# First attention stage: softmax weights made for two items at once, four buffers, the compressed branch and the weight split placed earlier

## The chip, the cores and the metric

The kernel runs on one core of one Trainium2 chip. The metric is the device time of one execution in microseconds (us), as the median of several runs. Engines are called by the profile's names or in words: PE is TensorE (PEld its weight loads), DVE is VectorE, ACT is ScalarE, POOL is GpSimd, SP issues the DMAs of the weight stream.

## The reference, cut to what matters

A model of four layers over 256 tokens of width 1024, all in float32: sparse attention, multi-head latent attention, a convolution layer and differential attention, with six feed-forward blocks. The change touches only the first mixer. There, 16 heads in 4 groups (head width 64) attend in three branches:

```python
s_c = einsum('bqghd,bjgd->bghqj', qb, k_cmp) * scale - slopes * (tf[:, None] - cmp_mid[None, :])
p_c = masked_softmax(s_c, cmp_end[None, :] <= t[:, None])          # 15 compressed blocks
o_c = einsum('bghqj,bjgd->bqghd', p_c, v_cmp)
...                                                                # selected branch o_s, window branch o_w
o = gb[..., 0:1] * o_c + gb[..., 1:2] * o_s + gb[..., 2:3] * o_w   # gates
return o.reshape(B, Q_BLOCK, NSA_HEADS * DH)
...
x = x + o @ w_out
```

k_cmp and v_cmp come from `compress`: 32 tokens with positions added, times w1, plus b1, gelu, times w2; k_cmp is then normed. With 256 tokens the selected and the window branch both see all earlier keys.

## The kernel before, in words

Every engine runs its own program in order; semaphores join them. All weights come as a stream of units of 3072 columns (piece a: 2048, piece b: 1024) into two slots of `raw`. ScalarE rounds a unit into `whi` (`hi_a`, `hi_b`) and VectorE takes the rest, raw minus hi, into `wlo` (`lo_a`, `lo_b`); TensorE multiplies three times (hi x hi, hi x lo, lo x hi) in `mm3`. Unit 10 is `U_OUT`, the first of three of the output projection; its operand is `hthi` and `htlo`, eight chunks of 128 rows, two heads each.

The first attention (`attention("nsa", ...)` on PE, ACT and DVE) is cut into 32 items, one for a head and a tile of 128 queries. `nsa_item(i)` gives head and tile: in each four, the first two are two heads with the first tile (128 keys, "short" below), the other two the same heads with the second tile (256 keys, "long"). An item goes: scores of both branches on TensorE (`nsa_scores`, two items at a time, four PSUM banks); `bias` on DVE adds slope times distance and finds the minimum (`near`, made by GpSimd per head); exp on ACT with the row sum (`lsum`); `probs` on DVE: reciprocal of two sums, product with two gates, scaling of both branches' weights; `transposes` on TensorE ("turning"); a copy on ACT into `n_pt`; `nsa_values` on TensorE for two items; and after each four a copy of the output (`post`, into `n_o`).

The loops on the three engines have index i. At i, DVE does bias(i) and probs(i-2); ACT does post, exp(i), the copy of item i-2; PE does, around transposes(i), scores of the pair two ahead and the values of the pair before. Tables (`besides`, `between`) written out by hand place other work at an index, after (on PE: before) that index's item work. In these tables are: the remaining keys and queries; the compressed branch, which is one chain over all three engines: hidden_taken, hidden_turned, hidden_biased, hidden_cubed, hidden_tanh, hidden_gelu, second_layer, key_root (a square root and two table loads), place_values, cmp_keys_normed, cmp_keys_turned, keys_placed, then for each tile t cmp_scores, cmp_biased, cmp_exp, cmp_weighted, cmp_turned, cmp_taken, and for each pair of chunks k cmp_values, branches_added, added_hi, added_lo; and the split of unit 10 (hi_a at 15, lo_a at 29). After the attention come cmp_values(3), the last additions and splits, and then TensorE waits until all eight chunks are split (`s_ol` at 8) before it starts unit 10. `busy` does nothing here (its count is 0).

The lines that the steps below touch: L681 exp, L690 copy of turned weights, L656 post, L797 hidden_biased, L808 to L810 key_root, L833 cmp_taken, L837 added_hi; L1342 transposes, L1377 scores, L1398 values, L1502 and L1505 second_layer, L1518 cmp_scores, L1540 cmp_values, L1037 to L1039 the projection; L1922 bias, L1954, L1955 and L1958 probs, L2079 to L2081 hidden_gelu, L2090 cmp_keys_normed; L465 near on GpSimd; L515 hi_a and L1708 lo_a.

## Time and profile before

| | |
|---|---|
| median of 3 runs | 1742.36 us (1740.43 to 1744.89) |
| the profiled execution | 1740.27 us, of which its span 1738.5 us |
| PE busy | 1666.1 us, 96% of the span |
| DVE, ACT, POOL busy | 1114.8, 809.4, 45.3 us |
| mean granted TensorE clock | 0.986 of full speed |
| first item's exp begins | 77.20 us |
| first matmul of the output projection | 163.97 us |
| stage between the two | 86.8 us, 5% of the span |

How to read it: an engine's row in a timeline has start, length, engine, line, operation, output and input and their sizes, the count merged, and in brackets how long the engine sat idle before and what released it. In the chain of work each row is start, length and what was running; the pieces follow each other until the end. Matmuls overlap, so that the distance between starts is less than a length. A clock of 0.5 means 1.2 GHz, 1.00 is 2.4 GHz.

### The profile page before, as it was taken

What the parts mean: (1) busy time and instruction counts of PE and PEld (TensorE: products, weight loads), DVE (VectorE), ACT (ScalarE), POOL (GpSimd) and SP (SyncE); (2) the same over time, 40 slices, a digit from 0 to 9 for tenths busy, and PEclk for the clock granted to TensorE, in tenths of its full rate; (3) what the DMA queues carried; (4) which work ended last, traced back from release to release, by engine and by line L of the source; (5) the groups of instructions that cost most, each with busy time, mean ns of one, the idle gap of its engine ahead of it and who ended that gap; (6) DMA issues with size and microseconds to landing.
All of it is one profiled execution on the core that took longest, in us unless ns stands there. A gap on an engine that the chain in (4) does not pass through costs nothing.

```text
span 1738.5 us, 30380 instructions
## 1 busy us (share of the span) xinstructions
PE 1666.1 (96%) x11793; PEld 1539.6 (89%) x11793; DVE 1114.8 (64%) x1735; ACT 809.4 (47%) x1236; POOL 45.3 (3%) x73
## 2 busy tenths in 40 slices
PE   8977999998999999999999999999999999899998
PEld 8856999987799999999997789999999999699997
DVE  4857766667666666766676476667666665676665
ACT  5575533346554334533352453335433354753333
POOL 0110000000000000000003010000000000000000
PEclk9988999998999999999999999999999999999999
DMA  7422454545046554444548255553555544045553
GB/s 268 161 71 86 166 197 181 183 155 179 28 147 230 215 217 181 182 181 181 184 162 243 71 191 191 191 190 141 201 184 190 191 166 150 17 167 203 189 187 145
DMA packets 56543, 293.92 MB, mean 169 GB/s; under 512 B 6720, under 2 KB 7232, under 8 KB 34080
## 3 DMA queue, kind: packets, MB, share of 16 engines
q1 hardware_dynamic: 52784, 280.61, 45.0%
q0 software_dynamic: 3696, 12.45, 2.4%
q8 instruction: 42, 0.69, 0.2%
q14 instruction: 21, 0.17, 0.0%
HBM read 290.95 MB, written 2.08 MB: 169 GB/s over the span
## 4 chain that ended last, share of the span: by engine, by line
PE 87%; DVE 6%; ACT 5%; issue 2%; DMA 0%; SPq 0%; DVEq 0%; ACTq 0%
PE bank L1037 18%; PE bank L1038 18%; PE bank L1039 18%; PE bank L1309 9%; PE bank L1278 4%; PE bank L1280 4%; PE bank L1282 4%; PE bank L1057 2%; PE bank L1608 1%; ACT att L704 1%; PE bank L1243 1%; PE bank L1245 1%; PE bank L1253 1%; PE bank L1342 1%; DVE wlo L1708 1%
## 5 line engine op out<-in xcount | busy, mean ns | idle before, releaser
L1037 PE MATMUL bank<-hthi,whi 128*128 128x256 f32 x2128 | 603.2, 283 | 2.1 <-DVE wlo L1714 2.1
L1038 PE MATMUL bank<-htlo,whi 128*128 128x256 f32 x2128 | 602.9, 283 | 0.0
L1039 PE MATMUL bank<-hthi,wlo 128*128 128x256 f32 x2128 | 602.9, 283 | 0.0
L1708 DVE TENSOR_TENSOR wlo<-raw,whi 128x2048 fp32r<-128x2048 f32 x171 | 391.8, 2291 | 96.4 <-ACT whi L515 96.4
L1037 PEld LDWEIGHTS bank<-hthi,whi 128*128 128x128 f32 x2128 | 408.7, 192 | 8.3 <-DVE wlo L1714 2.3
L1038 PEld LDWEIGHTS bank<-htlo,whi 128*128 128x128 f32 x2128 | 408.7, 192 | 4.7
L1039 PEld LDWEIGHTS bank<-hthi,wlo 128*128 128x128 f32 x2128 | 408.8, 192 | 0.0
L607 ACT ACTIVATE tr<-tr 128x256 f32<-128x256 f32 x132 | 55.1, 418 | 651.1 <-DVE tr L1801 651.1
L515 ACT ACTIVATE whi<-raw 128x2048 fp32r<-128x2048 f32 x171 | 326.4, 1909 | 31.0 <-PE bank L1039 29.2
L1801 DVE TENSOR_TENSOR tr<-bank,rb 128x512 f32<-128x512 f32 x132 | 91.2, 691 | 231.6 <-PE bank L1039 231.4
L1714 DVE TENSOR_TENSOR wlo<-raw,whi 128x1024 fp32r<-128x1024 f32 x171 | 208.4, 1219 | 22.0 <-ACT whi L523 21.3
L523 ACT ACTIVATE whi<-raw 128x1024 fp32r<-128x1024 f32 x171 | 178.2, 1042 | 0.4 <-PE bank L1039 0.3
L1037 PE MATMUL bank<-whi,hthi 128*128 128x384 f32 (+3 forms) x440 | 146.2, 332 | 8.0 <-DVE wlo L1714 3.7
L1038 PE MATMUL bank<-wlo,hthi 128*128 128x384 f32 (+3 forms) x440 | 144.3, 328 | 0.0
L1039 PE MATMUL bank<-whi,htlo 128*128 128x384 f32 (+3 forms) x440 | 144.2, 328 | 0.0
L1278 PE MATMUL bank<-whi,hidhi 128*128 128x512 f32 x288 | 113.3, 394 | 0.0
L1280 PE MATMUL bank<-wlo,hidhi 128*128 128x512 f32 x288 | 112.9, 392 | 0.0
L1282 PE MATMUL bank<-whi,hidlo 128*128 128x512 f32 x288 | 112.1, 389 | 0.0
L1804 DVE TENSOR_TENSOR tr<-tr 128x256 f32<-128x256 f32 x132 | 56.1, 425 | 63.8 <-ACT tr L607 63.8
L1309 PE MATMUL bank<-whi,hidhi 128*128 128x512 f32 x240 | 94.1, 392 | 0.0
L1309 PE MATMUL bank<-wlo,hidhi 128*128 128x512 f32 x240 | 94.1, 392 | 0.0
L1309 PE MATMUL bank<-whi,hidlo 128*128 128x512 f32 x240 | 93.4, 389 | 0.0
(281 smaller groups left out, 2004.2 us busy)
## 6 DMA issues: line engine op xcount, KB each, us to landing
raw<-in_stream SPq DMA_DIRECT2D x175, 1024.0 KB, 5.5
raw<-in_stream SPq DMA_DIRECT2D x176, 512.0 KB, 3.6
wide<-in_wide POOLq DMA_DIRECT2D x7, 512.0 KB, 4.1
tr<-in_taps POOLq DMA_DIRECT2D x6, 512.0 KB, 3.6
xn<-gated POOLq DMA_DIRECT2D x12, 142.0 KB, 3.0
proj<-gated POOLq DMA_DIRECT2D x8, 142.0 KB, 4.8
att<-gated POOLq DMA_DIRECT2D x8, 142.0 KB, 5.3
x<-in_x SPq DMA_DIRECT2D x2, 512.0 KB, 4.9
```

The costliest lines, as they stand in the source:

```text
L515: nc.scalar.activation(whi[:, s, 0:UA], raw[:, s, 0:UA], ACT.Copy).then_inc(s_hia, 1)
L523: nc.scalar.activation(whi[:, s, UA:UNIT], raw[:, s, UA:UNIT], ACT.Copy).then_inc(s_hib, 1)
L1037: nc.tensor.matmul(out, whi_, mhi, start=start, stop=False)
L1038: nc.tensor.matmul(out, whi_, mlo, start=False, stop=False)
L1039: return nc.tensor.matmul(out, wlo_, mhi, start=False, stop=stop)
L1278: nc.tensor.matmul(acc[2 * t + j][:, :], hidhi[:, b, lhs], whi[:, s, sl], start=start, stop=False, skip_group_check=True)
L1280: nc.tensor.matmul(acc[2 * t + j][:, :], hidhi[:, b, lhs], wlo[:, s, sl], start=False, stop=False, skip_group_check=True)
L1282: ins = nc.tensor.matmul(acc[2 * t + j][:, :], hidlo[:, b, lhs], whi[:, s, sl], start=False, stop=stop, skip_group_check=True)
L1309: ins = nc.tensor.matmul(acc[2 * t + j][:, :], a[:, 1, lhs], w[:, s, sl], start=False, stop=False, skip_group_check=True)
L1708: V.tensor_tensor(wlo[:, s, 0:UA], raw[:, s, 0:UA], whi[:, s, 0:UA].bitcast(F32), ALU.subtract)\
L1714: V.tensor_tensor(wlo[:, s, UA:UNIT], raw[:, s, UA:UNIT], whi[:, s, UA:UNIT].bitcast(F32), ALU.subtract)\
L1801: V.tensor_tensor(gu[:, j, :].rearrange("p (h n) -> p h n", h=2), gate_up_bank[j], both, ALU.mult)\
```

## The change

In the first attention alone:

- `n_sc` and `n_pr`, the buffers of biased scores and of weights, become four in place of three (short items get smaller ones), and every wait on them goes by four.
- `probs` of an item becomes `pair_probs` of two: one reciprocal over four sums and one product with four gates, then the four scalings; it runs at odd i for items i-3 and i-2.
- The compressed chain stands at earlier indices. The values of the second layer are copied once by ACT (`vraw`, ahead of them key_root), and GpSimd makes the four masked copies `vz`; they were made by ACT (`place_values`).
- Chunks 6 and 7 get the compressed branch by two more matmuls ahead of their own values in the same bank; their output goes directly to `hthi` (ACT) and `htlo` (DVE, `output_lo`). cmp_values(3) and branches_added(3) fall away. cmp_values of k uses one bank (`cbank`) and waits for the sum before it.
- Unit 10 is split in six pieces of 512 columns (`out_hi`, `out_lo`) inside the attention.
- TensorE waits before each chunk of unit 10 for that chunk alone.

The code that adds positions to the blocks (`blocks`, on DVE) is the same in both kernels.

```diff
-        n_sc = [att[:, a:a + 512].rearrange("p (b n) -> p b n", b=2) for a in (0, 512, 1536)]
-        n_pr = [att[:, a:a + 512].rearrange("p (b n) -> p b n", b=2) for a in (1024, 2048, 2560)]
+        n_sc = [att[:, a:a + w].rearrange("p (b n) -> p b n", b=2) for a, w in ((0, 256), (256, 256), (512, 512), (1024, 512))]
+        n_pr = [att[:, 1536 + a:1536 + a + w].rearrange("p (b n) -> p b n", b=2) for a, w in ((0, 256), (256, 256), (512, 512), (1024, 512))]
+        n_sums = lsum[:, 0, :].rearrange("p (i n) -> p i n", i=4)
+        vraw = xn[0:GJ, 0, 512:768]
...
-        n_stat = [slice(4 * i, 4 * i + 2) for i in range(3)]
+        n_stat = [slice(4 * i, 4 * i + 2) for i in range(4)]
...
                     for h in range(H1):
+                        if h == 10:
+                            pool.wait_ge(ev["vraw_ready"], 1)
+                            for q in range(HPG):
+                                ins = nc.gpsimd.tensor_scalar(vz[:, :, q, :], vraw.rearrange("p (g n) -> p g n", g=G1),
+                                                              cols[0:GJ, CO["pick"] + q:CO["pick"] + q + 1], None, ALU.mult)
+                            ins.then_inc(ev["vz_ready"], 1)
                         if h >= 4 and h % 2 == 0:
                             pool.wait_ge(s_bia, 2 * h - 4)
                         nc.gpsimd.tensor_scalar(near[:, h % 4, :], const[:, KO["causal"] + T:KO["causal"] + 2 * T],
...
                     if kind == "nsa" and i % 4 == 3:
                         act.wait_ge(s_pv, g + 1)
-                        nc.scalar.activation(n_o[:, i // 4, :], gub[0][:, 0:T], ACT.Copy).then_inc(s_raw, 1)
+                        if i // 4 < 6:
+                            nc.scalar.activation(n_o[:, i // 4, :], gub[0][:, 0:T], ACT.Copy).then_inc(s_raw, 1)
+                        else:
+                            nc.scalar.activation(hthi[:, i // 4, :], gub[0][:, 0:T], ACT.Copy).then_inc(s_oh, 1)
...
                             act.wait_ge(s_bia, i + 1)
-                            act.wait_ge(s_tr, item_round(kind, i - 3) + 1 if i >= 3 else RD[kind])
+                            act.wait_ge(s_tr, item_round(kind, i - 4) + 1 if i >= 4 else RD[kind])
...
-            def place_values(heads):
-                for h in heads:
-                    ins = nc.scalar.activation(vz[:, :, h, :], cbank[0:GJ, 256:256 + G1 * DH].rearrange("p (g n) -> p g n", g=G1),
-                                               ACT.Copy, scale=cols[0:GJ, CO["pick"] + h:CO["pick"] + h + 1])
-                return ins
+            def values_taken():
+                nc.scalar.activation(vraw, cbank[0:GJ, 256:256 + G1 * DH], ACT.Copy).then_inc(ev["vraw_ready"], 1)
...
+            def out_hi(q):
+                s = U_OUT % 2
+                if q == 0:
...
+                nc.scalar.activation(whi[:, s, q * 512:q * 512 + 512], raw[:, s, q * 512:q * 512 + 512], ACT.Copy).then_inc(s_outhi, 1)
+            def values_taken_and_rooted():
+                key_root()
+                values_taken()
...
             def cmp_taken(t):
                 act.wait_ge(ev[f"pc{t}_turned"], 1)
+                if t == 1:
+                    act.wait_ge(ev["vz_ready"], 1)
                 nc.scalar.activation(pct[t], cbank[0:GJ, :].rearrange("p (g n) -> p g n", g=G1), ACT.Copy).then_inc(ev[f"pct{t}"], 1)
...
             attention("nsa", {
                 3: lambda: k_copy(2), 5: lambda: k_copy(3), 7: lambda: q_copy(2), 9: lambda: (q_copy(3), hidden_taken()),
-                11: hidden_biased, 13: hidden_tanh, 15: lambda: hi_a(U_OUT), 16: lambda: (key_root(), place_values((0, 1))),
-                17: lambda: place_values((2, 3)).then_inc(ev["vz_ready"], 1), 19: keys_placed,
-                22: lambda: cmp_exp(0), 24: lambda: cmp_exp(1), 27: lambda: cmp_taken(0), 29: lambda: cmp_taken(1),
-                33: lambda: added_hi(0), 34: lambda: added_hi(1), 35: lambda: added_hi(2)})
-            added_hi(3)
+                10: hidden_biased, 11: hidden_tanh, 12: lambda: out_hi(0), 13: lambda: out_hi(1),
+                14: lambda: (values_taken_and_rooted()), 16: lambda: out_hi(2), 17: keys_placed, 18: lambda: cmp_exp(0),
+                19: lambda: out_hi(3), 20: lambda: cmp_exp(1), 22: lambda: cmp_taken(0), 23: lambda: cmp_taken(1),
+                25: lambda: out_hi(4), 26: lambda: out_hi(5), 27: lambda: added_hi(0), 29: lambda: added_hi(1),
+                30: lambda: added_hi(2)})
...
@@ -1384,19 +1409,27 @@
                     g, r = 2 * d, item_round(kind, 2 * d)
                     h, t = nsa_item(g)
                     c = h // 2
-                    if t == 0 and c >= 1:
+                    if t == 0 and 1 <= c < 7:
                         pe.wait_ge(s_raw, c)
+                    if t == 0 and c == 7:
+                        pe.wait_ge(s_ol, 7)
+                    if t == 0 and c == 6:
+                        pe.wait_ge(ev["vz_ready"], 1)
+                        pe.wait_ge(ev["pct1"], 1)
...
                     out = [gub[0][64 * m:64 * m + 64, t * P:(t + 1) * P] for m in range(2)]
+                    if c >= 6:
+                        for m in range(2):
+                            nc.tensor.matmul(out[m], vz[:, c // 2, (h + m) % HPG, :], pct[t][:, c // 2, :], start=True, stop=False)
...
                             ins = nc.tensor.matmul(out[m], p1[:, k, at:at + DH], n_pt[(g + m) % 4][:, j * P:(j + 1) * P],
-                                                   start=j == 0, stop=j == len(blocks) - 1)
+                                                   start=j == 0 and c < 6, stop=j == len(blocks) - 1)
...
                 else:
-                    pe.wait_ge(s_bia, 28 + k)
+                    pe.wait_ge(s_sum, k)
...
-                            ins = nc.tensor.matmul(n_add[k][64 * m:64 * m + 64, at:at + P], vz[:, c // 2, (2 * c + m) % HPG, :],
+                            ins = nc.tensor.matmul(cbank[64 * m:64 * m + 64, at:at + P], vz[:, c // 2, (2 * c + m) % HPG, :],
...
-                13: second_layer, 17: cmp_keys_turned, 19: lambda: cmp_scores(0), 21: lambda: cmp_scores(1),
-                25: lambda: cmp_turned(0), 27: lambda: cmp_turned(1), 29: lambda: cmp_values(0), 30: lambda: cmp_values(1),
-                31: lambda: cmp_values(2)})
-            cmp_values(3)
-            pe.wait_ge(s_ol, 8)
+                11: second_layer, 14: cmp_keys_turned, 16: lambda: cmp_scores(0), 17: lambda: cmp_scores(1),
+                19: lambda: cmp_turned(0), 21: lambda: cmp_turned(1), 23: lambda: cmp_values(0), 25: lambda: cmp_values(1),
+                27: lambda: cmp_values(2)})
             for u in range(U_OUT, U_OUT + 3):
-                step(u)
+                step(u, ready=(lambda k: pe.wait_ge(s_ol, k + 1)) if u == U_OUT else None)
...
-                    deep = 3 if kind == "nsa" else 2
+                    deep = 4 if kind == "nsa" else 2
                     if g >= deep:
                         dve.wait_ge(s_exp, g - deep + 1)
...
-                    if kind == "nsa":
-                        h, t = nsa_item(i)
-                        nk = P * (t + 1)
-                        own(V.reciprocal(pw[:, s, 0:2], lsum[:, 0, n_stat[i % 3]]))
-                        own(V.tensor_tensor(pw[:, s, 2:4], pw[:, s, 0:2], gates[:, t, 3 * h + 1:3 * h + 3], ALU.mult))
-                        for b in range(2):
-                            pr_ = n_pr[i % 3][:, b, 0:nk]
-                            ins = V.tensor_scalar(pr_, pr_, pw[:, s, 2 + b:3 + b], None, ALU.mult)
-                        ins.then_inc(s_prob, 1)
...
+                def pair_probs(d):
+                    s = d % 2
+                    h, t = nsa_item(2 * d)
+                    nk = P * (t + 1)
+                    dve.wait_ge(s_exp, 2 * d + 2)
+                    inverse, weight = (pw[:, s, a:a + 4].rearrange("p (i n) -> p i n", i=2) for a in (0, 4))
+                    own(V.reciprocal(inverse, n_sums[:, 2 * s:2 * s + 2, 0:2]))
+                    own(V.tensor_tensor(weight, inverse, gates[:, t, 3 * h:3 * h + 6].rearrange("p (i n) -> p i n", i=2)[:, :, 1:3],
+                                        ALU.mult))
+                    for m in range(2):
+                        for b in range(2):
+                            pr_ = n_pr[(2 * d + m) % 4][:, b, 0:nk]
+                            ins = V.tensor_scalar(pr_, pr_, pw[:, s, 4 + 2 * m + b:5 + 2 * m + b], None, ALU.mult)
+                        ins.then_inc(s_prob, 1)
...
-                        if 2 <= i <= cnt + 1:
-                            probs(i - 2)
+                        if i % 2 == 1 and 3 <= i <= cnt + 1:
+                            pair_probs(i // 2 - 1)
...
-                dve.wait_ge(ev["vz_ready"], 1)
+                dve.wait_ge(ev["vraw_ready"], 1)
...
+                                cbank[:, :].rearrange("p (c n) -> p c n", c=2), ALU.add).then_inc(s_sum, 1)
+            def output_lo(c):
+                dve.wait_ge(s_oh, c + 1)
+                V.tensor_tensor(htlo[:, c, :], gub[0][:, 0:T], hthi[:, c, :].bitcast(F32), ALU.subtract).then_inc(s_ol, 1)
+            def out_lo(q):
+                s = U_OUT % 2
+                dve.wait_ge(s_outhi, q + 1)
+                sl = slice(q * 512, q * 512 + 512)
+                ins = V.tensor_tensor(wlo[:, s, sl], raw[:, s, sl], whi[:, s, sl].bitcast(F32), ALU.subtract)
+                if q == 3:
+                    ins.then_inc(s_loa, 1)
+                if q == 5:
+                    ins.then_inc(s_lob, 1)
...
-                1: gates_from_tanh, 12: hidden_cubed, 14: hidden_gelu, 18: cmp_keys_normed, 21: lambda: cmp_biased(0),
-                24: lambda: (cmp_biased(1), cmp_weighted(0)), 26: lambda: cmp_weighted(1), 29: lambda: lo_a(U_OUT),
-                32: lambda: branches_added(0), 33: lambda: branches_added(1), 34: lambda: (branches_added(2), added_lo(0)),
-                35: lambda: added_lo(1)})
-            branches_added(3)
-            added_lo(2)
-            added_lo(3)
+                1: gates_from_tanh, 11: hidden_cubed, 12: hidden_gelu, 14: lambda: out_lo(0), 15: lambda: out_lo(1),
+                16: cmp_keys_normed, 18: lambda: cmp_biased(0), 19: lambda: out_lo(2), 20: lambda: (cmp_biased(1), cmp_weighted(0)),
+                22: lambda: cmp_weighted(1), 24: lambda: out_lo(3), 26: lambda: branches_added(0),
+                28: lambda: (branches_added(1), added_lo(0)), 29: lambda: out_lo(4), 30: lambda: (branches_added(2), added_lo(1)),
+                31: lambda: (added_lo(2), output_lo(6)), 32: lambda: out_lo(5), 35: lambda: output_lo(7)})
```

## Rows read from the trace of the kernel before

**Rows 1.** Page, costliest groups: busy us, mean ns, idle before them.

```profile
L1708 DVE TENSOR_TENSOR wlo<-raw,whi 128x2048 fp32r<-128x2048 f32 x171 | 391.8, 2291 | 96.4 <-ACT whi L515 96.4
...
L515 ACT ACTIVATE whi<-raw 128x2048 fp32r<-128x2048 f32 x171 | 326.4, 1909 | 31.0 <-PE bank L1039 29.2
```

**Rows 2.** Windows: length; PE, PEld, DVE, ACT, POOL busy; clock, DMA share, GB/s.

```profile
84.00:94.00 10.00, 10.00 (x100) 7.11 (x96) 6.48 (x37) 7.75 (x28) 1.70 (x2) 1.00 0.52 159
...
134.00:144.00 10.00, 9.79 (x64) 7.54 (x65) 7.57 (x37) 5.56 (x22) 0.85 (x1) 0.66 0.00 1
```

**Rows 3.** Timeline of ACT, items 7 and 16.

```profile
90.67 0.50 ACT L681 ACTIVATE att<-att,nmax 128x256 f32<-128x256 f32 x1
...
91.65 0.37 ACT L690 ACTIVATE proj<-bank 128x256 f32<-128x256 f32 x1
...
113.15 0.39 ACT L681 ACTIVATE att<-att,nmax 128x128 f32<-128x128 f32 x1
...
113.92 0.58 ACT L690 ACTIVATE wide<-bank 128x512 f32<-128x512 f32 x1
```

**Rows 4.** Timeline of DVE, bias and weights of single items.

```profile
104.05 0.42 DVE L1922 CUSTOM_DVE_ANT_0 att<-bank,proj 128x256 f32<-128x256 f32 x1
...
105.12 0.48 DVE L1958 TENSOR_SCALAR att<-att,pw 128x128 f32<-128x128 f32 x2
...
110.45 0.28 DVE L1922 CUSTOM_DVE_ANT_0 att<-bank,proj 128x128 f32<-128x128 f32 x1
...
110.87 0.16 DVE L1954 RECIPROCAL pw<-lsum 128x2 f32<-128x2 f32 x1
...
111.26 0.61 DVE L1958 TENSOR_SCALAR att<-att,pw 128x256 f32<-128x256 f32 x2
```

**Rows 5.** Chain of work, attention and first projection step: start, length, what.

```profile
100.67 0.93 ACT tr L797 x4
...
109.40 1.26 PE bank L1505 x16
...
114.71 1.28 ACT L563
...
127.42 1.91 PE bank L1518 x16
...
133.87 3.46 PE bank L1518 x16
...
160.64 1.04 PE bank L1540 x16
...
166.33 0.32 PE bank L1039
...
171.03 0.17 PE bank L1037
```

**Rows 6.** Timeline of DVE, side work with the wait ahead of it.

```profile
101.62 0.41 DVE L2073 TENSOR_TENSOR tr<-tr 128x240 f32<-128x240 f32 x1 [1.73 <-ACT tr L797]
...
106.26 0.28 DVE L2079 TENSOR_SCALAR tr<-tr 128x240 f32<-128x240 f32 x1 [0.65 <-ACT tr L803]
...
120.52 0.47 DVE L2090 TENSOR_SCALAR kcd<-bank,rs 60x64 f32<-60x64 f32 x2 [4.12 <-ACT xn L815]
```

**Rows 7.** Timeline of PE, turning at half clock, and the projection's first matmul.

```profile
104.19 1.11 PE L1342 MATMUL bank<-const,att 128*128 128x128 f32 x4 [2.61 <-DVE att L1958]
...
163.97 0.44 PE L1037 MATMUL bank<-whi,hthi 128*128 128x384 f32 x1 [2.31 <-DVE htlo L2126]
```

**Rows 8.** Timelines of DVE and POOL where a GpSimd instruction starts.

```profile
86.41 0.38 DVE L1955 TENSOR_TENSOR pw<-pw,gates 128x2 f32<-128x2 f32 x1
...
86.39 1.78 POOL L465 TENSOR_SCALAR proj<-const 128x256 f32<-128x256 f32 x2 [4.53 <-DVE nmax L1922]
```

**Rows 9.** Timeline of ACT, last side work of the compressed chain, last exp.

```profile
149.95 0.58 ACT L833 ACTIVATE xn<-bank 60x512 f32<-60x512 f32 x1
...
153.92 0.50 ACT L681 ACTIVATE att<-att,nmax 128x256 f32<-128x256 f32 x1
```

32 lines of the change are left out of this document (18 added, 14 removed).

## Prediction

> **What bounds the kernel now.** I read the chain of work first, then the stretch between 84 and 174 us by windows, then each engine's timeline there. Everything the diff touches lies in the first attention (32 items, from 77 us) and the first step of the output projection, which begins at 163.97 [rows 7]; nothing after that step changes. Items come in fours: two short (128 keys) and two long (256 keys). Up to about 97.7 us TensorE is full (10.00 of 10 us in 84 to 94); afterwards it isn't, and its granted clock falls, to a mean of 0.66 in 134 to 144 [rows 2], which is 1.2 GHz for most of it. What sets the pace there is the trip ScalarE, VectorE, TensorE and back.
>
> A ScalarE exp takes 0.77 for a short item (113.15 to 113.92) and 0.98 for a long one (90.67 to 91.65); the copy of the turned weights takes 0.37 or 0.58 [rows 3], of which the next start overlaps 0.1, so 0.3 or 0.5. On VectorE a bias step takes 0.42 (110.45 to 110.87) or 0.7 (two instructions of 0.42, overlapped), the reciprocal and the product 0.39 (110.87 to 111.26), the two scalings 0.48 or 0.61 [rows 4], with the next start at 0.40 or 0.53. Turning takes 0.44 (my estimate for two blocks, from 1.11 for four at half clock [rows 7]: 0.55 at most) or 0.6. So four items cost VectorE 2x0.42 + 2x0.7 + 4x0.39 + 2x0.40 + 2x0.53 = 5.66, and ScalarE 2x0.77 + 2x0.98 + 2x0.3 + 2x0.5 + 0.3 (taking the output) = 5.4. VectorE sets the pace, 1.42 an item; the rest of the stage is side work in the same in-order queues and the waits that it makes [rows 6].
>
> **Weights per two items.** One reciprocal and product in place of two saves 2x0.39 = 0.8 per four items: VectorE drops to 4.9. But the trip gets tighter. Before, between the exp of item i and the copy of item i, ScalarE has two further exps and two copies to do. Now the weights of both items of a pair wait for the pair's second exp, and ScalarE's copy of the first item comes after one more exp and copy alone. From that second exp to the copy: 0.39 + 0.48 + 0.44 + 0.1 between engines = 1.4 (short), 0.39 + 0.61 + 0.6 + 0.1 = 1.7 (long). ScalarE has 0.5 + 0.98 to fill the first, and 0.3 + 0.77 for the second: it idles 0.6 per four items. New pace 5.4 + 0.6 = 6.0, or 1.5 an item. So this edit saves VectorE time and gains nothing; from item 10 on, 21 items by 0.08 are 1.7 lost. The fourth place lets bias and exp run one item further ahead; with the copies in order behind them that shortens no step of the trip above. I take nothing, and the 1.7 just named as the most it could give back. Items 0 to 9 stay under TensorE's full queue: no change.
>
> **Second layer sooner.** From 97.8 the chain is: exp 10 and a copy 1.3, biases 0.93 [rows 5]; cubing 1.1 (I take it like the gelu), beside which ScalarE has exp 11, a post and a copy to do, 1.6; tanh 0.3; and the gelu, three instructions, 1.1 from the first's start at 106.26 in before [rows 6] to the next item's bias. That makes 103.05. In before the weights of items 10 and 11 went ahead of it. Now the bias of item 13 and the weights of item 10 stand behind it in VectorE's queue: 103.05 + 0.42 + 0.39 + 0.61 = 104.5. TensorE has by then been idle for 4.5 us, so I take half clock: turning 1.1 [rows 7], values 0.9, second layer (16 of its 20 matmuls took 1.26 while the clock rose [rows 5]; about 2.3 here, my estimate): 108.8; turning item 11, its copy, a piece of the split (0.5: 1909/4 ns [rows 1]), exp 14, a copy: 111.8. The root with its two table loads of 1.28 takes 3.2 [rows 5], the copy of the raw values 0.4: 115.4. Before, VectorE got them at 120.52 [rows 6]. The compressed chain is 5 ahead, but item 16's exp begins at 117.0 instead of 113.15 [rows 3], 4 behind.
>
> **Compressed scores.** 1.3 (post, exp 15), weights and turning 2.1, copy, piece, exp 17: 120.7; copy and placing keys: 122.0. Scores 1.9 [rows 5], biased 1.3: 125.3; bias, weights, turning: 127.3; values 1.05 and second scores 1.9, or 3.46 if the clock falls, as it did in before after a like gap [rows 5]; biased and weighted 2.7; item 18 at 135 to 136.6. The same steps on to the second turned tile, with 0.7 for outputs that ScalarE takes only after the values: 142.9 to 144.5; I take 143.7. In before it is taken by 150.5 [rows 9], with items up to 29 done by then. Seven sooner, but here items 24 to 31 are still to come.
>
> **Placing the values on GpSimd.** Four instructions, each at most 0.85 (the nearest, near, are twice the partitions: 1.78 for two [rows 8]), end by 119, and near for head 10 follows 0.9 later, at 120; item 20 needs it after 128. Hidden by 8 us. The trace shows what GpSimd costs VectorE: the product that starts with a GpSimd instruction takes 0.38 [rows 8], where reciprocal and product together take 0.39 otherwise [rows 4], so about 0.2 is lost in a meeting: 4x0.2 = 0.8 at most, and in a stretch where VectorE waits. I take 0.
>
> By the Trainium skill (SBUF — State Buffer, "SBUF: two separate sides"), VectorE and GpSimd hold the shared port pair exclusively for a whole instruction, so the loser blocks fully. By that, four instructions could cost 4x0.85 = 3.4 us; the row shows 0.2 for one meeting, so the trace bears out a short block and not a whole one.
>
> **The last eight items.** In this stretch I find the loss. cmp_values (1.05 each [rows 5]), branches_added, added_hi and added_lo (0.6 to 0.7 each, estimated from the split's 2.29 for four times the columns [rows 1]) now stand between items, and each waits for another queue. From 143.7, by the end of each pair's second exp: exp 24 and 25 and the copy between them put exp 25's end at +2.1. Its weights stand in VectorE's queue behind branches_added(0), which waits for cmp_values(0), which TensorE does after scores, turning and values of the pair before; with the bias of item 27 that is 1.8 late; exp 27, behind turning, a piece and the post, ends at +7.6. The next weights wait for added_hi(0), behind copy 25, behind turning 25, behind cmp_values(1), then comes 0.7 of added_lo: 2.4 late; exp 29 ends at +12.6. added_hi(1) likewise: 3.5 late; post(27) waits for the values, exp 31 ends at +19.9. Then weights 1.0, turning 0.6, values 0.8, turning 0.6, copy 0.5, values 1.25: +24.9, so the projection begins at 143.7 + 24.9 = 168.6. Natural pace would be 8x1.5 = 12.
>
> **Projection by chunk, split in pieces.** After its last values (160.57) before runs cmp_values(3), an add, a hi and a lo, 3.4 us until 163.97 [rows 5, 7]; from exp 31 (begun 153.92 [rows 9]) it is 10.0. Now exp 31's end to the first matmul takes 5.0. The values of item 28 now also wait for output_lo(6), since the bank is taken twice; by my count it is done 2 us earlier. Chunks 0 to 6 last 7x6x0.173 = 7.3 and cover chunk 7's hi and lo. Pieces: six of 0.5 on ScalarE for 1.9 before, six of 2.29/4 = 0.57 on VectorE for 2.29 [rows 1]: counted above where they hold an exp, else in idle time. The second split part (1.0 and 1.2) was covered by the step's first matmuls already and is worth 0. Before lost 11x(0.32 - 0.17) = 1.6 to half clock at the step's start [rows 5]; with gaps of up to 3 us ahead of it after, I expect the same, and keep -1.6 as a bound. The loads of unit 12 go out a few us sooner: 0. Positions were added by VectorE already; the diff doesn't touch them.
>
> **The sum.** 168.6 - 163.97 = +4.6. Against the profiled 1740.27 (span 1738.5) that is 1744.9. The median of the runs shown is 2.1 higher, 1742.36, which gives **1747.0**.
>
> **Rivals.**
> - *The tail is saved and nothing is given back* (faster). Place: items 24 to 31. If the values, adds and splits there fall into idle time, VectorE's 0.8 per four items counts over 21 items (4.2), with 3.4 of the tail and some of the 1.6: about -8, 1734. For it: in 134 to 144 VectorE has 2.4 and ScalarE 4.4 idle us [rows 2]. Against it: the waits are in queues, in the order above. It decides from exp 31 beginning before 154, as in before.
> - *TensorE falls to half clock in the last eight items* (slower). The TensorE work on that chain is about 0.6+1.05+0.6+1.1+1.05+0.4 and so on, 12.8 in all; 40% of it at half clock adds 5: 1752. For it: 0.66 in 134 to 144 with gaps of 2 to 3 us [rows 2]; I reckon gaps of 3 us. Against: in before cmp_values ran at full clock at 160.64 (1.04 for 16 matmuls [rows 5]) after gaps of the same kind.
> - *Splits come free and chain waits are shorter than I reckon*, so that the gains of the tail just meet the losses: 1742.
> - *GpSimd blocks VectorE fully*: +3.4 on the forecast, 1750.
>
> **Chances and range.** My forecast 0.50 (1743 to 1751 by itself; a third of it lies more than 0.3%, 5.2 us, above before; 0.3% is about what a measurement of this kernel can tell from no change), no give-back 0.22, half clock 0.18, even 0.06, GpSimd 0.04. Faster: 0.20 (most of the first rival). Slower: 0.17 + 0.16 + 0.03 = 0.36. Same: 0.44. The range takes in the forecast, the even case, and part of both outer ones: 1735 to 1754.
>
> **What would show it.** Right: four plain items take 6.0, with ScalarE waiting for turned long items; kcd is made near 115.5; item 16's exp near 117; exp 31 begins near 162; DVE waits for hthi (added_hi) inside the attention; the projection begins near 168.6 with no wait for a sum ahead of it. Wrong: exp 31 before 158, or TensorE at full clock from 104 on, which would take 2 to 3 us out of the two middle stretches, or VectorE waiting on GpSimd.

## The result, and the profile after

The changed kernel takes 1758.59 us (median of 4 runs, 1756.73 to 1761.16), beside 1741.39 us for the kernel before in the same rounds (1739.54 to 1744.89): ratio 1.0094, 95% interval 1.0072 to 1.0116. It is slower by 17 us, where +4.6 was forecast, and lies above the range.

Nearly all of it is in the stage that the change touches. Throughout I measure the *stage*: from the start of the first exp of the attention (item 0) to the first matmul of the output projection. It is 86.8 us before (77.20 to 163.97 [rows 7]) and 104.9 after (77.25 to 182.13): +18.1, of 20.0 between the two profiled executions (1740.27 and 1760.28). From that matmul to the end of the span it is 1574.5 before and 1576.4 after. Counting from the first exp matters, since it comes at 77.0 to 79.0 in the kernels below.

The costliest groups of the page after, against [rows 1]: the two big splits have one instruction less each, and the same duration.

```profile
L1739 DVE TENSOR_TENSOR wlo<-raw,whi 128x2048 fp32r<-128x2048 f32 x170 | 389.5, 2291 | 86.5 <-ACT whi L524 86.5
...
L524 ACT ACTIVATE whi<-raw 128x2048 fp32r<-128x2048 f32 x170 | 324.5, 1909 | 30.5 <-PE bank L1064 29.1
```

Windows of the kernel after, against [rows 2]:

```profile
84.00:94.00 10.00, 9.47 (x91) 6.66 (x92) 5.26 (x31) 7.27 (x27) 1.77 (x2) 1.00 0.51 159
94.00:104.00 10.00, 6.70 (x68) 4.71 (x64) 5.09 (x24) 8.10 (x31) 1.78 (x2) 1.00 0.43 159
104.00:114.00 10.00, 8.42 (x70) 6.96 (x72) 6.28 (x31) 4.91 (x16) 0.00 (x0) 0.66 0.01 2
114.00:124.00 10.00, 5.29 (x32) 3.47 (x29) 3.85 (x17) 8.24 (x25) 5.38 (x6) 0.69 0.00 0
124.00:134.00 10.00, 6.64 (x38) 5.84 (x38) 4.54 (x18) 2.09 (x8) 1.77 (x2) 0.50 0.01 2
134.00:144.00 10.00, 8.31 (x40) 6.32 (x41) 5.74 (x24) 4.15 (x16) 0.00 (x0) 0.50 0.00 0
...
164.00:174.00 10.00, 5.58 (x36) 3.45 (x32) 4.95 (x16) 4.47 (x14) 0.00 (x0) 0.50 0.00 0
174.00:184.00 10.00, 8.22 (x46) 6.20 (x47) 1.82 (x7) 3.07 (x5) 0.57 (x1) 0.50 0.16 54
```

The column to read is the granted clock (third from the end): four of these stretches of 10 us stand at 0.50, that is 1.2 GHz from end to end. None of the same stretches of the kernel before does; its lowest is this:

```profile
114.00:124.00 10.00, 4.40 (x31) 3.08 (x31) 4.30 (x23) 9.44 (x29) 1.70 (x2) 0.64 0.01 2
```

TensorE is busy 6.64 + 8.31 + 5.58 + 8.22 = 28.75 us in those four stretches of the kernel after. Had the same work run at 2.4 GHz, up to half of it, 14.4 us, would be gone. That is an estimate, and a rough one: the stretches with 0.66 and 0.69 hold more work at half clock, and the last one takes in 1.9 us of the projection.

What stands around the half clock is in its timeline (start, length, what; in brackets the idle time before, and what ended it), against [rows 5, 7]:

```profile
105.58 1.12 PE L1367 MATMUL bank<-const,att 128*128 128x128 f32 x4 [4.69 <-DVE att L2007]
...
117.44 0.27 PE L1544 MATMUL bank<-const,kcd 60*128 60x60 f32 x1 [2.96 <-DVE kcd L2127]
119.41 1.12 PE L1367 MATMUL bank<-const,att 128*128 128x128 f32 x4 [1.70 <-DVE att L2007]
...
123.82 3.62 PE L1551 MATMUL bank<-kcz,tr 128*128 128x30 f32 x16
130.81 0.69 PE L1367 MATMUL bank<-const,att 128*128 128x128 f32 x2 [3.36 <-DVE att L2007]
131.43 1.98 PE L1431 MATMUL bank<-wide,proj 128*64 128x128 f32 x16
133.33 3.62 PE L1551 MATMUL bank<-kcz,tr 128*128 128x30 f32 x16
...
160.99 0.66 PE L1367 MATMUL bank<-const,att 128*128 128x128 f32 x4 [2.08 <-DVE att L2007]
...
162.73 1.97 PE L1573 MATMUL bank<-xn 60*64 60x128 f32 x16
...
169.24 0.69 PE L1367 MATMUL bank<-const,att 128*128 128x128 f32 x2 [3.49 <-DVE att L2007]
...
182.13 0.69 PE L1062 MATMUL bank<-whi,hthi 128*128 128x384 f32 x1
```

All but one of the idle times shown are ended by L2007, the scalings of a *pair's* weights; the one at 117.44 is ended by the compressed keys (kcd). Among them the turning (L1367), both compressed scores (L1551) and one of the three compressed values (L1573, 162.73) run at half speed: 3.62 twice, for 1.91 in [rows 5], and 1.97 for 1.04. The order matters: the first scores are slow already, behind the idle 2.96 and 1.70, and the wait of 3.36 comes after them.

The longest wait, in VectorE's timeline:

```profile
118.51 1.78 DVE L2007 TENSOR_SCALAR att<-att,pw 128x256 f32<-128x256 f32 x4
...
127.58 0.40 DVE L2136 TENSOR_TENSOR tr<-wide,bank 128x240 f32<-128x240 f32 x1 [6.61 <-PE bank L1551]
...
128.89 0.42 DVE L1953 CUSTOM_DVE_ANT_0 att<-bank,proj 128x256 f32<-128x256 f32 x1
...
129.59 0.17 DVE L2001 RECIPROCAL pw<-lsum 128x4 f32<-128x4 f32 x1
```

and on ScalarE at the same time:

```profile
122.26 0.19 ACT L693 ACTIVATION_READ_ACCUMULATOR att<-att,nmax 128x1 f32 x1
...
131.53 0.39 ACT L702 ACTIVATE proj<-bank 128x256 f32<-128x256 f32 x1 [6.65 <-PE bank L1367]
```

The second exp of the pair 16, 17 ended at 122.45 (the read-out at 122.26). Its weights began at 129.59, 7.1 us later: in VectorE's queue they stand behind the biased compressed scores (L2136), which wait for TensorE's sixteen slow matmuls, and behind the bias of item 19. ScalarE and TensorE then stood still for 6.65 and 3.36 us.

### The profile page after: what moved, and what is told of

It reads as the page before. It is cut to its first block, busy times and chain, and to the rows that moved or that the text cites. A ratio compares the mean times of both kernels' runs of the same rounds, so it can differ in the third digit from the quotient of the medians.

```text
span 1758.5 us, 30297 instructions
## 1 busy us (share of the span) xinstructions
PE 1678.5 (95%) x11793; PEld 1548.0 (88%) x11793; DVE 1111.1 (63%) x1707; ACT 807.7 (46%) x1236; POOL 49.4 (3%) x77
## 3 DMA queue, kind: packets, MB, share of 16 engines
HBM read 290.95 MB, written 2.08 MB: 167 GB/s over the span
## 4 chain that ended last, share of the span: by engine, by line
PE 87%; DVE 6%; ACT 5%; issue 2%; DMA 0%; SPq 0%; DVEq 0%; ACTq 0%
PE bank L1062 18%; PE bank L1064 18%; PE bank L1063 18%; PE bank L1334 9%; PE bank L1303 4%; PE bank L1305 4%; PE bank L1307 4%; PE bank L1082 2%; PE bank L1639 1%; PE bank L1367 1%; ACT att L716 1%; PE bank L1073 1%; PE bank L1431 1%; PE bank L1268 1%; PE bank L1270 1%
## 5 line engine op out<-in xcount | busy, mean ns | idle before, releaser
L1334 PE MATMUL bank<-whi,hidlo 128*128 128x512 f32 x240 | 93.4, 389 | 0.0
```

The source lines that it names most:

```text
L1334: ins = nc.tensor.matmul(acc[2 * t + j][:, :], a[:, 1, lhs], w[:, s, sl], start=False, stop=False, skip_group_check=True)
```

## Experiments

Each kernel ran several times (4 to 12) in turn with the kernel before on the same chip; ratios are to that, with the 95% interval. They ran in three groups of four, each on another chip: `a_warm`, `b_warm`, `a_single`, `b_pair` (the kernel before took 1744.8 us beside them), `b_pair_warm`, `b_four`, `a_single_warm`, `a_pair_early` (1744.7), and the remaining four (1744.1).

How finely these numbers tell: a stage is read from one kept execution of a kernel. Up to item 28 `a_single_end` below does the same work as `a_single`, and its exp 14 comes 30.8 us after its first exp, for 31.9 there, so that 1 us of stage can be spread. Times of the kernel before spread more, from 1736.6 to 1752.8 us at mean granted clocks from 0.989 to 0.977, and its kept trace is of an execution of 1740.27, below the medians beside these runs. So times and stages need not agree to better than some 4 us.

### Fillers: what TensorE's clock costs

In TensorE's idle stretches fillers were put ahead of its waits: matmuls of finished weights into a bank that the next turning overwrites. They change no result, and keep the clock up. `a_warm` is the changed kernel with them, `b_warm` the kernel before.

```diff
                     g, r = base + i, item_round(kind, i)
-                    pe.wait_ge(s_prob, g + 1)
                     bank_free(r)
+                    if kind == "nsa":
+                        fill(FILL.get(i, 0), tp[r % 2])
+                    pe.wait_ge(s_prob, g + 1)
```

with FILL = {10: 30, 13: 18, 14: 8, 16: 20, 18: 8, 20: 4, 22: 4, 24: 6, 26: 14, 28: 22, 30: 12} in `a_warm`, {11: 14, 16: 22, 20: 10, 28: 14} and 12 ahead of the projection in `b_warm`.

> The changed kernel with filler matmuls (128x256, result thrown away) ahead of turning steps at which TensorE sat idle: 30 ahead of item 10, 18 of 13, 8 of 14, 20 of 16, 8, 4, 4, 6 ahead of 18, 20, 22, 24, 14 of 26, 22 of 28, 12 of 30; at full clock one takes about 0.12 us. Theory 1 (half clock is what the forecast missed): the granted clock stays near 1.00 from 104 to 184, the projection's first matmul comes at 166 to 170 instead of 182.2, and the time falls by 12 to 16 us, to about 1744. Theory 2 (the in-order waits between the engines are longer than summed, the clock being a by-product): first matmul within 4 us of 182, time within 4 us of 1758.6.

> The kernel before with the same kind of filler: 14 ahead of turning item 11, 22 ahead of 16, 10 ahead of 20, 14 ahead of 28, 12 ahead of the projection. Theory 1: half clock cost this kernel about 7 us of its stage plus 1.6 at the projection's start (second layer and items 11 to 13 about 2, scores of items 20 and 21 about 2, the second compressed scores and what stands about them about 3), so 5 to 9 us faster, about 1734. Theory 2: within 2 us of before.

Measured: `a_warm` 1744.69 us, ratio 1.001 (0.9992 to 1.0028), stage 91.4 for 104.9: theory 1. `b_warm` 1734.44 us, ratio 0.995 (0.9927 to 0.9973), stage 83.7 for 86.8. Its time fell as theory 1 said or more; the stage gave 3.1 of the 7 that were expected of it. Windows of `a_warm`:

```profile
104.00:114.00 10.00, 8.50 (x92) 7.39 (x91) 7.59 (x38) 7.03 (x23) 0.00 (x0) 1.00 0.01 2
124.00:134.00 10.00, 8.58 (x75) 7.29 (x74) 7.28 (x28) 3.71 (x13) 1.77 (x2) 1.00 0.00 0
134.00:144.00 10.00, 8.80 (x68) 6.66 (x68) 8.24 (x40) 6.46 (x22) 1.78 (x2) 0.83 0.15 32
154.00:164.00 10.00, 8.92 (x92) 7.32 (x91) 6.61 (x23) 5.10 (x16) 0.00 (x0) 1.00 0.01 2
```

and its timeline of TensorE; L1073 are fillers, L1558 the compressed scores:

```profile
122.32 1.97 PE L1558 MATMUL bank<-kcz,tr 128*128 128x30 f32 x16 [1.15 <-ACT kcz L846]
124.12 2.63 PE L1073 MATMUL bank<-whi 128*128 128x256 f32 x20
127.65 0.44 PE L1374 MATMUL bank<-const,att 128*128 128x128 f32 x2 [0.89 <-DVE att L2014]
...
170.10 0.45 PE L1062 MATMUL bank<-whi,hthi 128*128 128x384 f32 x1
```

The scores take 1.97 again. What follows: 13.5 us of the changed kernel's stage, and 13.9 of its time (14.6 by the ratios), are TensorE's half clock. Before, it cost at least 3.1 of the stage, and some 1.6 at the start of the projection [rows 5]; that is 4.7 of the 10.4 us by which the median fell, and where the rest lies one trace of each doesn't tell. Neither kernel with fillers is at full clock throughout: `a_warm` has 0.83 from 134 to 144, `b_warm` 0.77, 0.89 and 0.83 in the three stretches from 114 to 144. With that said, the waits by themselves leave +7.7 of stage (91.4 against 83.7).

### Which part makes the waits: the weights per two items

`a_single` is the changed kernel with the weights item by item again; everything else of the change stays. `b_pair` is the kernel before with four places and the weights per pair, and nothing else of the change. `b_four` has the four places alone.

```diff
-                        if i % 2 == 1 and 3 <= i <= cnt + 1:
-                            pair_probs(i // 2 - 1)
+                        if 2 <= i <= cnt + 1:
+                            one_probs(i - 2)
```

(`one_probs` is what `probs` did before, with four places; `b_pair` has this edit the other way round.)

> The changed kernel with the weights made item by item again, at index i for item i-2, with four places kept and everything else as changed. Theory 1 with the tight trip (pairs make TensorE's gaps): the gap before turning item 10 shrinks from 4.7 to about 3 us because its weights go ahead of the gelu, VectorE pays 0.8 per four items, and the projection's first matmul comes 5 to 9 us earlier (173 to 177). Theory 3 (the new order of the compressed chain and of the adding makes the gaps, and pairs matter little): within 3 us of 182.

> The kernel before with four places and weights per two items, nothing else changed. Tight trip: first matmul 2 to 8 us later than 163.97 (1.7 by the pace, the rest by items' weights that come behind side work and by half clock), time 1743 to 1750. If pairs pay (VectorE's queue sets the pace): 3 to 4 us earlier, 1738. If pairs matter little: within 2 us of before.

> The kernel before with four places for scores and weights, weights item by item. All theories: the place is no step of the trip, so first exp to first projection matmul within 2 us of 86.8 and the time within 2 us of before. If the fourth place lets exp run ahead over side work: 2 to 5 us shorter.

| kernel | time, us | ratio (95%) | stage, us |
|---|---|---|---|
| `a_single` | 1736.8 | 0.9952 (0.9934 to 0.997) | 83.0 |
| `b_pair` | 1761.29 | 1.0091 (1.007 to 1.0113) | 108.55 |
| `b_four` | 1740.81 | 0.9996 (0.9969 to 1.0023) | 85.7 |

Of the expectations, that for `b_four` held by its stage (1.1 shorter) and its ratio. Those for the other two were missed by every theory: the first projection matmul of `a_single` came at 161.69, for 173 to 177 or about 182, and that of `b_pair` at 185.74, for 172 at the latest.

The weights per pair cost 21.9 us of stage in the changed kernel (104.9 against 83.0) and 21.8 or 22.9 in the kernel before (108.55 against 86.8, or 85.7 with four places). By the ratios of the times it is 25 us in the first and 16 in the second. They are more than the whole loss: the rest of the change gains 0.5%, and the fourth place alone can't be told from nothing. In the kernel before the longest wait sits elsewhere than in the changed one. TensorE's timeline of `b_pair`:

```profile
129.50 0.69 PE L1343 MATMUL bank<-const,att 128*128 128x128 f32 x2 [7.87 <-DVE att L1987]
```

It is the same pair, items 16 and 17. Item 16's exp ends at 120.6 and item 17's at 125.9, since ScalarE has the root and the placing of the values between them, and the weights begin at 128.29, behind the compressed keys (kcd, 127.21). There the wait for the second exp is the larger part. In `a_single`, VectorE's timeline at the place of the 7.1 us wait reads:

```profile
118.57 0.15 DVE L2000 RECIPROCAL pw<-lsum 128x2 f32<-128x2 f32 x1
...
118.96 0.48 DVE L2004 TENSOR_SCALAR att<-att,pw 128x128 f32<-128x128 f32 x2
122.63 0.40 DVE L2149 TENSOR_TENSOR tr<-wide,bank 128x240 f32<-128x240 f32 x1 [3.19 <-PE bank L1551]
```

The weights of item 16 are made before VectorE goes to wait for the compressed scores, so TensorE has that item to turn and multiply with beside them. Its own timeline shows it:

```profile
120.52 1.97 PE L1551 MATMUL bank<-kcz,tr 128*128 128x30 f32 x16
122.33 0.42 PE L1367 MATMUL bank<-const,att 128*128 128x128 f32 x2
122.68 1.09 PE L1431 MATMUL bank<-wide,proj 128*64 128x128 f32 x16
123.97 1.97 PE L1551 MATMUL bank<-kcz,tr 128*128 128x30 f32 x16 [0.20 <-DVE tr L2152]
...
161.69 0.69 PE L1062 MATMUL bank<-whi,hthi 128*128 128x384 f32 x1
```

### Pairs and clock together

`b_pair_warm` is `b_pair` with fillers, `a_single_warm` is `a_single` with fillers.

```diff
+            FILL = {10: 30, 12: 20, 16: 50, 20: 18, 22: 8, 24: 6, 28: 16}      # b_pair_warm, and 12 ahead of the projection
+            FILL = {11: 18, 13: 16, 16: 6, 18: 6, 20: 4, 28: 10, 30: 10}       # a_single_warm
```

> The kernel before with four places and weights per two items, plus filler matmuls ahead of the turning steps where the run without them idled (30 ahead of item 10, 20 of 12, 50 of 16, 18 of 20, 8 of 22, 6 of 24, 16 of 28, 12 ahead of the projection). It splits the 21.7 us that pairs cost. If half clock is most of it: first exp to first projection matmul 93 to 97 us (108.6 without filler, 86.8 before), total 1745 to 1749. If the waits behind side work are most of it: 102 to 107 us, total 1754 to 1760.

> The changed kernel with weights item by item, plus filler matmuls (18 ahead of turning item 11, 16 of 13, 6 of 16, 6 of 18, 4 of 20, 10 of 28, 10 of 30). If the two causes are independent parts, half clock gives back what it cost here: 3 to 6 us below the run without filler (stage 83.0), so stage 77 to 80 and the time about 1731 to 1734. If the clock is a small matter once the pairs are gone: within 2 us of it.

Measured: `b_pair_warm` 1746.92 us, ratio 1.0021 (1.0003 to 1.0039), stage 93.4. `a_single_warm` 1737.01 us, ratio 0.9964 (0.9943 to 0.9985), stage 84.6. So with TensorE warm the pairs cost 9.7 in the kernel before (93.4 against 83.7) and 6.8 in the changed one (91.4 against 84.6). The other 12 to 15 of the 22 us are the half clock that the pairs' waits bring. Without pairs the fillers bring the changed kernel nothing (84.6 for 83.0, the time equal). They can stand in the way:

```profile
106.83 3.02 PE L1073 MATMUL bank<-whi 128*128 128x256 f32 x18
109.69 0.60 PE L1374 MATMUL bank<-const,att 128*128 128x128 f32 x4
```

The 18 fillers (L1073) of `a_single_warm` run ahead of item 11's turning, whose weights had been ready since 104.92; its exp 14 comes 2.4 us later than that of `a_single`, counted from the first exp.

### Place in the queue, or the wait for the second exp

`a_pair_early` calls a pair's weights one place sooner in VectorE's order: ahead of one piece of side work and the bias that follows it. They still wait for the pair's second exp. `a_early_warm` adds fillers to it, FILL = {10: 20, 12: 12, 14: 8, 16: 16, 18: 10, 20: 4, 22: 4, 24: 4, 26: 8, 28: 14, 30: 10}.

```diff
-                        if i % 2 == 1 and 3 <= i <= cnt + 1:
+                        if i % 2 == 0 and 2 <= i <= cnt:
                             pair_probs(i // 2 - 1)
```

> The changed kernel with the pair's weights made at index 2d+2 in place of 2d+3, still for both items at once and after the second one's exp. If the weights' place in VectorE's queue (behind one more bias and one more piece of side work) is what costs: the stage falls from 104.9 to 88 to 94 us, time 1741 to 1748. If waiting for the second exp is what costs: 100 to 105 us, time 1754 to 1759.

> The changed kernel with a pair's weights one place earlier in VectorE's order (stage 87.8, 1742.6 us), and filler matmuls in TensorE's idle stretches of the stage. Theory A (the half clock's price grows with the waits, so that with the pair early little of it is left): stage 85 to 87, time down by 1 to 2 us. Theory B (the half clock costs 13 us of any such stage): stage near 80. What is left over the 83.0 of the weights item by item is the wait for the second exp.

Measured: `a_pair_early` 1742.64 us, ratio 0.9991 (0.9969 to 1.0013), stage 87.8. `a_early_warm` 1741.7 us, ratio 0.9985 (0.9969 to 1.0001), stage 86.75. One place sooner gives back 17.1 of the 21.9 us. VectorE's timeline of `a_pair_early`, same place:

```profile
123.61 0.18 DVE L2001 RECIPROCAL pw<-lsum 128x4 f32<-128x4 f32 x1 [2.30 <-ACT att L693]
...
127.06 0.40 DVE L2136 TENSOR_TENSOR tr<-wide,bank 128x240 f32<-128x240 f32 x1 [2.16 <-PE bank L1551]
```

The weights wait for ScalarE's exp alone, and the compressed scores come behind them. The 4.8 that remain over `a_single` (87.8 against 83.0) are what the pair costs in the sooner place. Its first item still waits for the second's exp, and what stands behind the weights now waits with them: the weights of items 14 and 15 begin at 117.45, after 4.88 us of waiting for exp 15, and kcd, whose input is ready more than a microsecond sooner, is made behind them at 119.74. Counted from the first exp that is 4.0 later than in `a_single`, and TensorE stands idle for 6.52 us before it. Fillers bring 1.05 us of stage here (theory A's bounds were 85 to 87), where they brought 13.5. The granted clock is 1.00 with them in each stretch of ten from 104 to 164 but 114 to 124, where it stays at 0.66.

### The rest of the change, without the pairs

`a_single_all` lets the projection wait for all eight low halves of its operand; `a_single_act` lets ScalarE place the compressed values, as before, in place of GpSimd, two beside the root at index 14 and two at 15; `a_single_end` has fillers only near the end (12 and 16 ahead of items 28 and 30, 12 ahead of the projection).

```diff
-                step(u, ready=(lambda k: pe.wait_ge(s_ol, k + 1)) if u == U_OUT else None)
+                if u == U_OUT:
+                    pe.wait_ge(s_ol, 8)
+                step(u)
```

```diff
-                            for q in range(HPG):
-                                ins = nc.gpsimd.tensor_scalar(vz[:, :, q, :], vraw...)
...
                 key_root()
-                values_taken()
+                place_values((0, 1))
...
-                dve.wait_ge(ev["vraw_ready"], 1)
+                dve.wait_ge(ev["vz_ready"], 1)
```

> The changed kernel with the weights item by item (stage 83.0), and the projection waits for all eight low halves of its operand before its first matmul, instead of for each as it comes to it. Theory A (beginning by chunk is where the rest of the change gains): the first matmul comes 2 to 3 us later than at 161.7 and the time rises by 2 to 3 us, to 1739 or 1740. Theory B (the gain of the rest is the compressed chain and the adding out of the tail; the projection reaches its last chunk late enough anyway): the first matmul moves by 1 us or less, time 1737 to 1738.

> The changed kernel with the weights item by item (stage from the first exp of the attention to the first matmul of the projection 83.0 us, 1736.8 us), and the compressed values placed by ScalarE in four scalings from the bank, as before, in place of one copy by ScalarE and four scalings by GpSimd; kcd waits for them again. Theory A (GpSimd's placing is worth what ScalarE no longer does): before, each of the four took ScalarE about 0.5 us, so that ScalarE carries 1.5 us more between exps 15 and 17 and kcd is about 1.5 us later, while the scaling by VectorE beside GpSimd (1.78 for 1.14) is short again: stage 83 to 85. Theory B (the placing by GpSimd costs more than it saves, through VectorE's longer scalings): stage 81 to 83, time down by 1 us or more.

> The changed kernel with the weights item by item, and filler matmuls in TensorE's idle stretches near the end of the attention alone: 12 and 16 ahead of the probabilities' turning of items 28 and 30, and 12 ahead of the projection's first matmul. Theory A (the projection's first 3 us run at the half clock, 0.32 us a matmul for 0.17, and fillers there give that back): the first matmul stays at about 161.7 and the time falls by 1 to 2 us, to 1735 or 1736. Theory B (fillers delay as much as they warm, as they did all through the stage): 1737.

| kernel | time, us | ratio (95%) | stage, us |
|---|---|---|---|
| `a_single_all` | 1739.23 | 0.997 (0.9948 to 0.9992) | 85.35 |
| `a_single_act` | 1738.82 | 0.9975 (0.9958 to 0.9991) | 85.3 |
| `a_single_end` | 1738.1 | 0.9969 (0.9951 to 0.9988) | 82.0 |

In `a_single_all` the stage is 2.35 longer, as theory A said, but only a part of that is the edit's. TensorE's timeline of `a_single_all`:

```profile
155.90 1.12 PE L1367 MATMUL bank<-const,att 128*128 128x128 f32 x4 [1.27 <-DVE att L2006]
...
164.07 0.69 PE L1062 MATMUL bank<-whi,hthi 128*128 128x384 f32 x1 [0.97 <-DVE htlo L2178]
```

and of `a_single`, at the same turning:

```profile
155.98 0.66 PE L1367 MATMUL bank<-const,att 128*128 128x128 f32 x4 [1.35 <-DVE att L2004]
```

The wait for the last low half, which the edit makes, is 0.97. The last values before it end 1.3 later than in `a_single`, though exp 31 begins 0.1 sooner, since turning and values from 155.90 on ran at half clock in this execution and at full clock, for a time, in that of `a_single`. The edit stands behind them and can't have done that. So beginning by chunk is worth 1.0 of stage as far as shown, and the intervals of the two times overlap.

With the values back on ScalarE the stage is 85.3, 0.3 above theory A's 83 to 85 and outside theory B's 81 to 83. Counted from the first exp, kcd is made 1.9 later than in `a_single` and exp 17 comes 1.8 later; at exp 31, 0.9 of it is left, and the other 1.4 come behind exp 31, at half clock as in `a_single_all`. So placing them on GpSimd is worth some 1 to 2 us of stage, at the limit of what one trace tells; here too the intervals of the times overlap. What GpSimd costs VectorE is there, but is smaller than what ScalarE is spared.

`a_single_end` is undecided between its theories. Its first matmul comes at 159.04 and at full clock,

```profile
159.04 0.34 PE L1062 MATMUL bank<-whi,hthi 128*128 128x384 f32 x1
```

and its stage is 1.0 shorter; but it was 1.0 ahead of `a_single` at exp 14 already, long before its first filler, and so the fillers gave the stage nothing that shows. The projection's start is some 1.5 us shorter. The time doesn't show it: its ratio's interval overlaps that of `a_single`, and in the profiled execution 1578.7 us pass from that matmul to the span's end, where in `a_single` it is 1573.8. Differences of 1 or 2 us between two of these kernels are at the limit of what so many runs tell.

Both `b_warm` (1734.4 us) and `a_single` (1736.8 us) beat the kernel before by about half a per cent. Which of the two is better is not told by their intervals.

## Why the prediction was wrong

The direction held (more slow than fast, +4.6), the size did not (+18.1 of stage, +17 of time). Step by step:

**Weights per two items: the step that failed.** It was priced at 1.7 us, from the trip that starts at the pair's second exp. That trip was set up as if VectorE took the weights at once. By the order of the calls it takes them only after the next bias *and* the side work between, each of which can wait for TensorE, while the side work waits for matmuls that TensorE does before it turns the pair. Measured: 21.8 to 22.9. The parts by experiment, in the changed kernel: 17.1 for the place in the queue with what it brings, 4.8 for what is left one place sooner, the wait for the second exp in it. The sum was not built from that 1.7 but by walking the stage, and the walk did put weights behind side work: behind branches_added in the last eight items (1.8 late), and behind the biased compressed scores, 5.3 us after exp 17 (120.7 to 125.3, and a bias), where 7.1 were measured. It charged the first to the adding and gave the second no price, and neither to the pairs; `b_pair`, for which I then expected 2 to 8 us, shows that they are the pairs'.

**TensorE's half clock: the term missing from the sum.** It stood as a rival with a chance of 0.18 and a price of 5. It is what took the kernel out of the range, and costs 13.5 of stage; the sum had half clock only at item 10, the second layer and in the upper value of the second scores. Two things were wrong. The price counted 12.8 us of TensorE's work in the last eight items at 40%. The rows after have 28.75 us of busy TensorE in stretches granted 0.50, half of them around the compressed scores. (That the 14.4 us of that count lie close to the 13.5 measured is partly luck, since it leaves out the stretches that are only in part at 0.50.) And against it stood that the compressed values ran at full clock before after like gaps. The length of a gap alone doesn't decide: in the kernel before, the work after an idle 2.69 (152.11) ran at full clock, in the kernel after the clock fell within 2 us of an idle 2.08 (160.99). The gaps themselves were reckoned nearly right, 4.69 for 4.5 at item 10 and 3.49 for 3 in the last eight. What was not reckoned is how much work then runs slow, and that a slow TensorE makes the next wait longer: VectorE's wait for the first scores is 6.61 after and 4.17 in `a_warm`. From which of these stretches the 13.5 come is not shown by stretch.

**Sum with the clock kept up.** With most of the half clock taken out, the sum of the terms was near: 168.6 forecast for the first matmul from a first exp at 77.2, a stage of 91.4, and `a_warm` has 91.4. That it agrees to the tenth is luck. Up to the second turned tile `a_warm` takes 64.4 from its first exp (143.15 in its trace), 2.1 less than the 66.5 forecast, and from there to the projection 26.9, 2.1 more than the 24.9; the sum also held some half clock, and `a_warm` holds what the fillers delay. Against the changed kernel itself the terms agree less well. The second turned tile is taken 5.8 late in the trace after (start 149.50, forecast 143.7), and exp 24 to the first matmul takes 32.2 (149.97 to 182.13; forecast 24.9 from the tile). In `a_warm` the latter is 26.5. Exp 31 begins at 172.81, where I named "near 162" as a sign of being right; its end to the first matmul is 8.3 after and 5.6 in `a_warm`, where 5.0 was forecast. ScalarE's timeline, against [rows 9]:

```profile
149.50 0.58 ACT L858 ACTIVATE xn<-bank 60x512 f32<-60x512 f32 x1
149.97 0.40 ACT L693 ACTIVATE att<-att,nmax 128x128 f32<-128x128 f32 x1
...
165.78 0.60 ACT L702 ACTIVATE wide<-bank 128x512 f32<-128x512 f32 x1 [2.74 <-PE bank L1367]
...
172.81 0.50 ACT L693 ACTIVATE att<-att,nmax 128x256 f32<-128x256 f32 x1
```

**The loss in the last eight items: wrong cause in the main.** I gave it to branches_added, added_hi and added_lo between the items. All of these stay in `a_single`, where exp 24 to the first matmul takes 22.9, less than the 25.9 of the kernel before, which has other side work there. In the changed kernel it is 32.2. So 9.3 of it come with the pairs and their clock. What the adding costs by itself no run shows.

**Second layer sooner.** Near: kcd was made at 116.92 (forecast 115.4) and item 16's exp began at 118.22 (forecast 117.0, before 113.15 [rows 3]). The compressed chain is sooner and the items later, as said.

**GpSimd: near zero, in the right direction.** The timeline of GpSimd after:

```profile
116.91 3.68 POOL L469 TENSOR_SCALAR xn<-xn,cols 60x256 f32<-60x256 f32 x4 [19.91 <-ACT xn L826]
```

Four scalings of VectorE that began inside it took 1.78 (118.51, above), and the same four take 1.14 elsewhere (149.77 in this trace): 0.64 lost, on the path, for the 0 I took and the 0.8 I bounded it by. The 1.78 stands again in `a_warm` and `a_pair_early`. By the Trainium skill (SBUF — State Buffer, "SBUF: two separate sides") the loser of the shared port pair blocks for the whole instruction of the other, where VectorE's instruction is in a two-port mode or has two SBUF inputs. Which mode these scalings run in, no run here shows. The rows show a slowing of 0.64 in all, for four scalings that lie wholly beside GpSimd's work, and no block of the length of one of its instructions (0.92).

**Projection by chunk.** Worth 1.0 as far as `a_single_all` shows. The half clock at the step's start stayed as expected, 12 matmuls at 0.32 from 182.13 on.

**The rival of no give-back** comes near what the change does without its pairs: `a_single` gains 0.5%, 8 us, as the rival said. Half of that rival's gain, though, was VectorE's saving by pairs (4.2), which `a_single` doesn't have, and the stages show only 3.8 (86.8 to 83.0). The agreement of the sizes is no proof of its mechanism.

Not settled: how the 2.7 between `b_four` (85.7) and `a_single` (83.0) divides. Chunks and GpSimd's placing, undone alone, cost 1.0 and some 1 to 2, with a spread of 1 us in each stage. The split in six pieces and the sooner second layer weren't run by themselves.

## What to carry to other kernels

Where several engines hand small pieces round in in-order queues, an operation that is merged over two items is priced by where it then stands in its queue: list everything between its last input and its turn, and what each of those waits for. Merging saved VectorE 0.2 us an item here and cost 22 us; the same merge one place sooner cost 5. And a stage in which TensorE waits 2 to 5 us at a time is priced at both levels of the clock, over all of TensorE's work in it: here the loss was 7.7 us of stage with fillers and 18.1 without.

## What the runs showed of the hardware that I had not expected

- Waits of VectorE and TensorE feed each other through the clock: 7.7 us of longer waits with fillers that keep the clock up (91.4 against 83.7) became 18.1 us of stage as run (104.9 against 86.8).
- Useless matmuls in idle stretches made the kernel before 0.5% faster (ratio 0.995, 0.9927 to 0.9973) with no other change. In `a_single` they gained nothing.
- The length of an idle stretch alone didn't tell whether TensorE's clock fell: full clock after 2.69 us in the kernel before (152.11), half clock after 2.08 in the changed one (160.99 to 162.73).
- A GpSimd instruction beside VectorE's scalings of 256 columns stretched four of them from 1.14 to 1.78 us.
